# Seven places for weight sets in the first feed-forward phase, and another order of stores and ring loads

## The reference

```python
def swiglu(x, w_in, w_out):                      # w_in 1024 x 5632, w_out 2816 x 1024
    gate, up = jnp.split(x @ w_in, 2, axis=-1)
    return (jax.nn.silu(gate) * up) @ w_out

h = layer_norm(DEEPNORM_ALPHA * h + m, ln_mix_g[layer], ln_mix_b[layer])
f = swiglu(h, ffn_w_in[layer], ffn_w_out[layer])
h = layer_norm(DEEPNORM_ALPHA * h + f, ln_ffn_g[layer], ln_ffn_b[layer])
```

## Time and profile before

| | us |
|---|---|
| median of three runs | 3021.66 (3021.19 to 3023.3) |
| the profiled execution's own time | 3015.59 |
| its span, first to last instruction | 3013.8 |
| PE busy (86% of the span) | 2591.7 |
| DVE busy (59%) | 1783.2 |
| ACT busy (30%) | 916.2 |
| POOL busy (28%) | 843.9 |

### The profile page before, as it was taken

One profiled execution on the slowest core, in us unless ns is written; L12 is line 12 of the kernel. 1 busy time (PEld: TensorE's weight loads), 2 busy tenths in 40 slices (PEclk: granted clock), 3 DMA queues, 4 the chain that ended last, 5 costly groups with the idle time before them and its releaser, 6 DMA issues. The chain is left out here.

```text
span 3013.8 us, 39934 instructions
## 1 busy us (share of the span) xinstructions
PE 2591.7 (86%) x12860; PEld 2141.8 (71%) x12860; DVE 1783.2 (59%) x3085; ACT 916.2 (30%) x1462; POOL 843.9 (28%) x606
## 2 busy tenths in 40 slices
PE   6786799878778689988999999987988778778996
PEld 5676677766566578866888888876866656557885
DVE  8889248444344348673667766665744434344778
ACT  3233241322122226323223222231132222223532
POOL 3878202343243240022111111100234234335002
PEclk8989899989889899999999999998998988989998
DMA  4333221355454468732111011103035445446763
GB/s 138 94 102 86 88 98 47 90 163 154 126 165 141 135 190 289 227 119 69 36 36 35 21 35 35 35 14 140 8 105 167 138 142 163 128 143 213 264 213 133
DMA packets 442288, 355.97 MB, mean 118 GB/s; under 512 B 30272, under 2 KB 376512, under 8 KB 438464
## 3 DMA queue, kind: packets, MB, share of 16 engines
q1 hardware_dynamic: 442176, 354.52, 38.2%
HBM read 296.31 MB, written 58.13 MB: 118 GB/s over the span
## 5 line engine op out<-in xcount | busy, mean ns | idle before, releaser
L1050 DVE TENSOR_TENSOR s5o_w_sets<-s5o_w_sets_plain,s5o_w_sets 128x512 fp32r<-128x512 f32 x140 | 105.0, 752 | 267.0 <-ACT s5o_w_sets L62 266.5
L1050 DVE TENSOR_TENSOR hgo_w_sets<-hgo_w_sets_plain,hgo_w_sets 128x512 fp32r<-128x512 f32 x140 | 108.1, 774 | 261.2 <-ACT hgo_w_sets L62 260.6
L2442 PE MATMUL ps<-aT_hi,w_hi 128*128 128x512 f32 x624 | 251.5, 403 | 4.3 <-DVE hg_q_raw L2703 2.5
L614 PE MATMUL ps<-aT_hi,hgo_w_sets 128*128 128x512 f32 x640 | 217.3, 417 | 43.8 <-DVE hgo_w_sets L1050 43.8
L614 PE MATMUL ps<-aT_hi,s5o_w_sets 128*128 128x512 f32 x640 | 217.1, 417 | 40.0 <-DVE s5o_w_sets L1050 40.0
L62 ACT ACTIVATE s5o_w_sets<-s5o_w_sets_plain 128x512 fp32r<-128x512 f32 (+1 forms) x173 | 116.1, 680 | 431.8 <-POOL s5o_w_sets_plain L1275 363.4
L62 ACT ACTIVATE hgo_w_sets<-hgo_w_sets_plain 128x512 fp32r<-128x512 f32 (+1 forms) x173 | 116.0, 680 | 429.4 <-POOL hgo_w_sets_plain L1275 358.7
L2442 PE MATMUL ps<-aT_hi,w_lo 128*128 128x512 f32 x624 | 246.1, 394 | 0.0
L2442 PE MATMUL ps<-aT_lo,w_hi 128*128 128x512 f32 x624 | 244.8, 392 | 0.0
L2414 POOL TENSOR_TENSOR w_lo<-w_raw_plain,w_hi 128x1024 fp32r<-128x1024 f32 x38 | 91.7, 2420 | 526.6 <-ACT w_hi L62 526.6
L1275 POOL TENSOR_TENSOR s5o_w_sets_plain<-s5o_w_sets_plain 128x512 f32<-128x512 f32 x100 | 144.0, 1448 | 305.9 <-DMA s5o_w_sets_plain<-in_ffn_w_in_dram 305.9
(11 more groups left out here) (416 smaller groups left out, 6211.5 us busy)
## 6 DMA issues: line engine op xcount, KB each, us to landing
s5o_w_sets_plain<-in_ffn_w_in_dram SPq DMA_DIRECT2D x208, 256.0 KB, 3.4
hgo_w_sets_plain<-in_ffn_w_in_dram SPq DMA_DIRECT2D x208, 256.0 KB, 3.4
w_raw_plain<-in_hg_w_in_dram SPq DMA_DIRECT2D x40, 512.0 KB, 3.9
aT_hi_plain<-in_ffn_w_out_dram SPq DMA_DIRECT2D x68, 256.0 KB, 4.4
s5o_w_sets_plain<-in_ffn_w_in_dram SPq DMA_DIRECT2D x96, 128.0 KB, 4.2
hgo_w_sets_plain<-in_ffn_w_in_dram SPq DMA_DIRECT2D x96, 128.0 KB, 4.1
s5o_hidden<-s5o_home_plain SPq DMA_DIRECT2D x11, 1024.0 KB, 5.6
hgo_hidden<-hgo_home_plain SPq DMA_DIRECT2D x11, 1024.0 KB, 5.6
```

The lines of the kernel that those rows point to most:

```text
L614: ins = t.matmul(ps[:, 4 * second + to, :], w[:, kk, :], x_sets[x][xs][:, kk, :], start=(kk == 0 and m == 0), stop=(kk == 3 and m == 2))
L1050: v.tensor_tensor(lo, plain_rows(pos)[1], hi.bitcast(F32), ALU.subtract).then_inc(S["set_lo"], 1)
L2442: ins = t.matmul(ps[:, half, :], w[b][:, kk, :], x[:, kk, cols], start=(kk == 0 and q == 0), stop=(kk == KT - 1 and q == 2))
```

## The change

Home 3, a block of the size of two places that lies unused in the first phase, becomes the seventh place for a weight set. So `SLOT_AT` is `n % 7`, and since 14 is twice 7, every set takes a place used seven products earlier. SP loads positions 7 to 13 and then 0 to 6 of the next iteration, with `store_late` of the iteration before behind position 1 and `store_early` behind position 2. In the last iteration the six plain sets of tile 21 take the places in that same order, inside the iteration. On POOL, the four hidden sums stand further back among the set sums. In the second phase, the first pairs in the slots are loaded as each is freed by a plain product and not after the last of them; the pairs of steps 66 to 68 go to home 0, 1 and 2 and are loaded ahead of the wait for `first_weights`; the high and low parts of pairs 1 and 2 stand ahead of the second half of tile 21's activation and product.

```diff
+    SETS = SLOTS + 1
-    SLOT_AT = [n % SLOTS for n in range(2 * NP)]
+    SLOT_AT = [n % SETS for n in range(2 * NP)]
-    FREED_BY_PART = [5, 2, 6, 4, 7, 8]
+    FREED_BY_PART = [5, 2, 6, 4, 7, 8, 1]
...
     def plain_slot(n, last):
-        return (2 * NP + n) % SLOTS if last else n
+        return n
...
-        return 1 + i * SLOT_AT.count(slot) + SLOT_AT[:pos + 1].count(slot)
+        return int(slot < SLOTS) + i * SLOT_AT.count(slot) + SLOT_AT[:pos + 1].count(slot)
...
     def plain_rows(pos):
+        if SLOT_AT[pos] == SLOTS:
+            return plain_homes[3][:, 0:4 * P], plain_homes[3][:, 4 * P:8 * P]
...
-    LAST_RING = RING[6:8] + RING[0:6] + [("home", 0), ("home", 1), ("home", 2)]
+    LAST_RING = [("home", 0), ("home", 1), ("home", 2)] + RING[6:8] + RING[0:6]
...
-            for pos in (1, 3, 2, 0, 4, 5):
+            for pos in (1, 3, 2, 0, 4, 5, 6):
                 load_set(0, pos)
             def body(i):
                 final = isinstance(i, int) and i == LAST - 1
-                for pos in range(SLOTS, 10):
+                for pos in range(SETS, 2 * NP):
                     load_set(i, pos)
-                if not (isinstance(i, int) and i == 0):
-                    store_late(i - 1)
-                for pos in range(10, 2 * NP):
-                    load_set(i, pos)
-                s.wait_ge(S["merged"], (2 * i + 1) * NMERGE)
-                carry(s, i)
-                store_early(i, early_hidden)
-                if not final:
-                    for pos in range(SLOTS):
-                        load_set(i + 1, pos)
+                for n in range(SETS):
+                    if final and n < SLOTS:
+                        s.wait_ge(S["product"], index(i, 2 * NP - SETS + n) + 1)
+                        load_plain(n, True)
+                    elif not final:
+                        load_set(i + 1, n)
+                    if n == 1 and not (isinstance(i, int) and i == 0):
+                        store_late(i - 1)
+                    if n == 2:
+                        s.wait_ge(S["merged"], (2 * i + 1) * NMERGE)
+                        carry(s, i)
+                        store_early(i, early_hidden)
...
-            for n in range(4):
-                s.wait_ge(S["product"], index(LAST - 1, 2 * NP - SLOTS + n) + 1)
-                load_plain(n, True)
             store_late(LAST - 1)
-            for n in range(4, 6):
-                s.wait_ge(S["product"], index(LAST - 1, 2 * NP - SLOTS + n) + 1)
-                load_plain(n, True)
...
-            s.wait_ge(S["part"], 16)
             for n in range(EARLY_RING, LAST):
+                if n < EARLY_RING + 3:
+                    s.wait_ge(S["part"], 8 + max(FREED_BY_PART[2 * (n - EARLY_RING):2 * (n - EARLY_RING) + 2]))
                 load_pair(n)
...
+            for n in range(LAST_STEPS, LAST_STEPS + 3):
+                load_pair(n)
             s.wait_ge(S["out_acc"], accs_before(5))
             for to, of in first_weights:
                 s.dma_start(to, of).then_inc(S["next_loaded"], 16)
-            for n in range(LAST_STEPS, STEPS):
+            for n in range(LAST_STEPS + 3, STEPS):
                 load_pair(n)
...
             def body(i):                       # POOL
-                if not first:
-                    hidden_sum(i - 1, 0)
-                    hidden_sum(i - 1, 1)
-                make_sum(i, 5)
-                if not first:
-                    hidden_sum(i - 1, 2)
-                make_sum(i, 6)
+                for n, pos in enumerate((5, 6, 7, 8, 9)):
+                    make_sum(i, pos)
+                    if n >= 2 and not first:
+                        hidden_sum(i - 1, n - 2)
                 if not first:
                     hidden_sum(i - 1, 3)
-                for pos in (7, 8, 9, 12, 13):
-                    make_sum(i, pos)
+                make_sum(i, 12)
+                make_sum(i, 13)
```

More of the change, by code:

```diff
@@ L217, in project_and_feed @@
         "stats", "chain", "normed", "centred", "rescaled", "scaled", "turned", "hi", "lo", "x_copy", "x_sum", "x_set_hi", "x_set_lo",
-        "set_in0", "set_in1", "set_in2", "set_in3", "set_in4", "set_in5", "set_sum", "set_hi", "set_lo",
+        "set_in0", "set_in1", "set_in2", "set_in3", "set_in4", "set_in5", "set_in6", "set_sum", "set_hi", "set_lo",
         "product", "kept", "merged", "silu_late", "silu_early", "early_stored", "late_stored", "hidden_sum",
@@ L283, in set_rows @@
     def set_rows(pos):
+        if SLOT_AT[pos] == SLOTS:
+            return homes[3][:, 0:4 * P], homes[3][:, 4 * P:8 * P]
         return slots[:, SLOT_AT[pos], 0, :], slots[:, SLOT_AT[pos], 1, :]
     def plain_rows(pos):
+        if SLOT_AT[pos] == SLOTS:
+            return plain_homes[3][:, 0:4 * P], plain_homes[3][:, 4 * P:8 * P]
         return plain_slots[:, SLOT_AT[pos], 0, :], plain_slots[:, SLOT_AT[pos], 1, :]
@@ L420, in load_set @@
                 f, r = tile_at(i, pos)
-                if isinstance(i, int) and i == 0 and pos < SLOTS:
+                if isinstance(i, int) and i == 0 and pos < SETS:
                     s.wait_ge(S["part"], FREED_BY_PART[pos])
@@ L921, in _ @@
             half_silu(True, 0)
-            pair_hi(0)
+            for n in range(EARLY_RING):
+                pair_hi(n)
             half_silu(True, 1)
-            for n in range(1, STEPS):
+            for n in range(EARLY_RING, STEPS):
                 pair_hi(n)
@@ L1236, in _ @@
             half_product(True, 0)
-            pair_lo(0)
+            for n in range(EARLY_RING):
+                pair_lo(n)
             half_product(True, 1)
-            for n in range(1, STEPS + 1):
+            for n in range(EARLY_RING, STEPS + 1):
                 if n < STEPS:
                     pair_sum(n)
-                if n > 1:
+                if n > EARLY_RING:
                     pair_lo(n - 1)
```

## The result

The changed kernel takes 2695.24 us (median of 4 runs, 2692.92 to 2696.5), the kernel before 3021.43 us beside it. The ratio is 0.8919, with a 95% interval from 0.8903 to 0.8934. The forecast was 2693 us, in a range from 2676 to 2750. The profiled execution took 2695.05 us where that of before took 3015.59, so 320.5 us less; the sum of the prediction was 329.

The account below looks back on a forecast made before the run. The prediction took a latency at two positions of the first phase as the bound. Gains of 310.3 + 7 + 12 = 329 us left 2686.6 of 3015.59 us; with 6.07 us for the median, 2693 us, range 2676 to 2750.

Parts of the forecast that it names:

- The bound: First phase: PE idles on latency at positions 0 and 1, 8.6 us against one product in between, 2.74 us.
- The way of 8.6 us: First phase: time from a product's end to the start of one taking its place; 6.8 us where POOL and DVE don't collide.
- Seventh place: First phases of both feed-forwards: six products between uses leave no gap, gaining 156.9 + 153.4 = 310.3 us.
- 7.9 us to spare: First phase with seven places: six products in between cover 16.5 us against a way of 8.6 us.
- The walk through POOL, ACT, DVE and SP: One first-phase iteration: each engine's order and load followed in time, none holding PE up; all loads below 38.4 us.
- a rival (18%): First phase: late landings behind stores or ACT's order leave gaps of 1 to 5 us an iteration, say 2745 us; 18%.
- Between the phases: From first to second phase: weight loads leave SP's queue, gaining 3.5 us each time, between 0 and 4.1; 7 us.
- Pairs 1 and 2 ahead: Start of second phase: their loads and splits ahead of tile 21's second half cost 0, at worst 2 us each time.
- End of the second phase: Sums and low parts fill DVE's idle time before step 66: 5.2 us, first feed-forward 7; 12 us, between 0 and 17.
- DVE held up by POOL: First phase rival: POOL instructions prolong DVE's, up to 2853 us, 5%; `set_lo` mean over 0.9 us would be its sign.
- The DMA load: First phase: 28 loads and three stores fit in 14 products, needing 28 of 38.4 us; DMA share about 0.7.

Follow-up runs that it names:

- late_0_1: Changed kernel with the loads of positions 0 and 1 in the first phase waiting five products longer than their place asks for: 3039.99 us.
- places_alone: Kernel before with the seventh place alone, all orders, pairs and the second phase's ring as before: 2712.99 us, ratio 0.8976.
- late_2: Changed kernel with every first-phase load issued two products later than its place is free, four products in between in place of six: 2708.16 us.
- pairs_before: Changed kernel with pairs 1 and 2 split behind the second half again, one wait for all plain parts ahead of pair 3's load: 2693.09 us, ratio 0.8914.
- ring_before: Changed kernel with steps 66 to 76 in the ring places of the kernel before, no load ahead of the wait for the accumulations: 2708.73 us, ratio 0.8953.
- order_alone: Kernel before, on its six places, with the change's new orders of stores, hidden sums, pairs and ring: 3036.13 us, ratio 1.0051.

## Why the prediction was right

**The bound** was named rightly: a latency at two positions, not a rate. late_0_1 shows it from one side (two waits bring all of the gaps back), places_alone from the other (the place alone takes them all away). One reading of the chain was slightly off: behind 2531.34 the product of position 0 still runs, 2.74 us, and PE then stands idle for 5.83 us, not from 2531.34 on. The way of 8.6 us and the sum don't depend on it.

**Seventh place: 310.3 us.** Measured 155.7 + 154.0 = 309.7. The product of 2.744 us was 2.747.

**7.9 us to spare** was too much. The way of 8.6 us is that of a load which lands in 3.2 to 3.6 us; behind the late stores a load of the same size took 7.72, and the way 11.70. Against six products, 16.5 us, 4.8 are left. The term did not suffer, but a kernel with four products in between (late_2) already loses. The walk through POOL, ACT, DVE and SP named each engine's order rightly and left out what a store does to the load behind it. The prediction had that effect only as a rival (18%), at 5.1 us of data in front of the load; measured it is 7.72 against 3.3, so 4.4 us, and it fits into the time to spare.

**Between the phases: 7 us.** Measured 1.9 + 2.8 = 4.7, inside the bounds of 0 to 4.1 each. The weight loads left the queue as I said. In the second feed-forward, of their 4.06 us the issue of the two rows took back 0.99 (0.79 + 1.19 against 0.56 + 0.43) and the landing of the early store 1.02 (7.00 against 5.98), and the last load of pair 0 landed 0.76 earlier (3.19 against 3.95): 2.8. PE was done with the plain products earlier, and only waited the longer for pair 0: 5.31 us in place of 2.44 in the first feed-forward, 4.25 in place of 3.97 in the second. Pairs 1 and 2 ahead cost 0, and pairs_before agrees.

**End of the second phase: 12 us.** Measured 6.5 + 3.3 = 9.8 against before, and 12.7 against ring_before. In the second feed-forward I took 5.2, three whole sums, and the idle time before the step in hi 0 did shrink by 5.06 us, from 8.50 to 3.44. But its load was issued 172.1 us after the start of the phase in place of 170.6 (2630.60 - 2458.49; before 2946.92 - 2776.3), and the next two idle times grew from 0.65 + 0.54 to 0.46 + 1.56 us: 5.2 - 1.5 - 0.8 = 2.9. I had taken the times at which that place comes free and its loads land as fixed. The place came free later because PE's first 36 matmuls of the phase took 11.09 us in place of 9.61 (2458.49 to 2469.58; before 2776.29 to 2785.90), the first twelve of them at the lower clock: that is the 1.5 us.

The first feed-forward gave nearly the 7 that I took, but not by my reckoning. DVE's idle times of 7.72 + 1.22 + 0.65 us there shrank to 0.47 + 0.29. The hold beside POOL's split for the next stage did not go: a `pair_lo` now takes 5.09 us in place of 1.22, where a sum took 4.36 in place of 0.69; it only fell into time in which DVE had stood idle. Together that is 8.6 us, and PE's first twelve matmuls, 5.29 us in place of 3.05, took 2.2 back. That the two sizes met is luck.

**The sum** of the three is 324.2 us; the first phase started 3.1 us later in this execution (555.5 against 552.4; other kernels here have 553.5 to 558.6), and 0.6 us were lost at the very end, which makes the 320.5. Against the prediction's 329 that is 8.5 us too little. The forecast of the median is nearer, 2693 against 2695.24, because it adds the 6.07 us by which the median of before lay above its profiled execution, and in the changed kernel the two are 0.2 us apart. This part of the hit is luck; the term that carries it, 310.3 of 329, is not.

**DVE held up by POOL** was a rival at 5%, and its sign came: the mean of `set_lo` is 1.07 us over all places, not under 0.9. DVE's rows in order of time, and below them POOL's:

```profile
2252.51 0.67 DVE L1078 TENSOR_TENSOR hgo_act_out<-hgo_act_out,ps 128x512 f32<-128x512 f32 x1
...
2253.93 0.68 DVE L1055 TENSOR_TENSOR hgo_w_sets<-hgo_w_sets_plain,hgo_w_sets 128x512 fp32r<-128x512 f32 x1
...
2259.65 1.78 DVE L1055 TENSOR_TENSOR hgo_w_sets<-hgo_w_sets_plain,hgo_w_sets 128x512 fp32r<-128x512 f32 x1
...
2270.26 0.68 DVE L1055 TENSOR_TENSOR hgo_w_sets<-hgo_w_sets_plain,hgo_w_sets 128x512 fp32r<-128x512 f32 x1
```
```profile
2251.99 1.76 POOL L1339 TENSOR_TENSOR hgo_home_plain<-hgo_home_plain 128x512 f32<-128x512 f32 x1
2253.92 1.84 POOL L1339 TENSOR_TENSOR hgo_home_plain<-hgo_home_plain 128x512 f32<-128x512 f32 x1 [0.18 <-POOL hgo_home_plain L1339]
...
2259.06 1.83 POOL L1281 TENSOR_TENSOR hgo_w_sets_plain<-hgo_w_sets_plain 128x512 f32<-128x512 f32 x1 [3.29 <-DMA hgo_w_sets_plain<-in_ffn_w_in_dram]
```

The `set_lo` at 2259.65, behind the start of a POOL sum, takes 1.78 us, and the one at 2270.26, with none beside it, 0.68. The one at 2253.93 took 0.68 too with a POOL sum beside it, and that sum took 1.84 in place of 1.30: either of two that meet can be the one that is prolonged. The prediction took DVE alone to pay. Over an iteration it is 12 x 0.36 us, some 4.3 of the 14.9 us that DVE had to spare against PE, so it decides nothing; places_alone, with 30 us less of DVE time in the phase, is no faster in it. The Trainium skill ("SBUF — State Buffer", Who interferes with whom) has it that a DVE instruction with at most one SBUF input, outside its 2-port modes, does not contend with GpSimd. The trace agrees: the merge step at 2252.51, with one input in PSUM, took 0.67 us with a POOL sum beside it.

**The DMA load.** The 28 loads and three stores of 14 products ran in 38.4 us at a DMA share of 0.69, as the rows had it. The time for one DMA that the prediction takes from the Trainium skill ("DMA: Bandwidth & Descriptors", Anatomy of one DMA) is given there for DMAs issued from GpSimd, and those here are issued by SP, so it does not speak of them; no term of the sum used it.

**Not tried:** what the gaps would be with six places in an unbroken turn, five products between all uses. By the way of 11.7 us in late_2 it would have had 13.7 us, so by this estimate no gap and the gain of the first phase without a seventh place.

## What to carry to other kernels

Where buffers are used in turn, look at the shortest distance between two uses of one place, and not only at their number: here six places with two positions at a distance of two lost 155 us a phase, and a seventh that made all distances equal gave all of it back. Reckon the way from free to filled with the slowest landing in the loop, which is that of the load behind the largest store, not with the median. An order that is free while places are ample can cost 3 to 6% of a phase when they are short, and two such edits don't add up (14 and 33 us alone, 17 together), so each is to be tried on the buffer count that it will run with.

## What was not expected of the hardware

A 256 KB load issued 0.8 us behind stores of 0.5 and 1 MB landed after 7.72 us in late_2 in place of 3.3, and one at the same place in order_alone after 7.60; with stores of a quarter the size eight of the nine waits for a set were gone. A DVE subtraction with both inputs in SBUF rose from 0.69 to as much as 1.83 us beside a POOL sum, and a POOL sum from 1.30 to 1.84; how often they meet moved DVE's busy time in a phase by 30 us (248.84 and 278.64) with the same instructions. Behind 5.31 us without a matmul PE's first twelve took 5.29 us at a granted clock of 0.50; behind 2.44 us they took 3.05 at 1.00.
